# A two-block layer on one core: the last gate summed ahead of the expert gathers, the vector work around them rearranged

## The chip, the cores and the metric

The kernel runs on one core of a Trainium2 chip. The core has a matrix engine (TensorE, PE in the profile), a vector engine (VectorE, DVE), an engine for activation functions (ScalarE, ACT), a general one (GpSimd, POOL), and SyncE (SP), which here only issues transfers. Each runs its own list of instructions in order; semaphores order them against each other. 16 DMA engines move data between HBM and the on-chip memory. The metric is device microseconds of one execution, median of several.

## The reference, cut to what matters

Two transformer blocks over 256 tokens of width 1024, all in float32. The change touches the end of the first block, where a learned gate `gt2` scales the output of a mixture of tiny experts, and the first lines of the second:

```python
mod = (silu(c) @ w_mod + b_mod)               # one row of 6 x 1024
sh1, sc1, gt1, sh2, sc2, gt2 = jnp.split(mod, 6)
h = rmsnorm(x, ln_mix_g) * (1 + sc1) + sh1    # block 1: attention and convolution
...
x = x + gt1 * (mixed @ w_out)
h2 = rmsnorm(x, ln_ffn_g) * (1 + sc2) + sh2
x = x + gt2 * peer_ffn(h2, ...)
x = rmsnorm(x, ln_final_g)
h = rmsnorm_2(x, pre_norm_w)                  # block 2
q, k, v, ... = jnp.split(h @ w_in_2, ...)

def peer_ffn(xn, w_q, sub_keys, expert_u, expert_v):
    s = einsum('bshpd,hpkd->bshpk', q, sub_keys)      # scores of 2 x 128 half keys, 8 heads
    v_half, i_half = top_k(s, 16)                     # then the 16 best of the 256 sums
    experts = i1 * 128 + i2                           # 8 x 16 = 128 experts a token
    act = gelu(einsum('cd,ced->ce', xc, expert_u[ec]))
    return einsum('ce,ced->cd', softmax(top_s) * act, expert_v[ec])
```

## The kernel before, in words

The kernel is one program for five queues. Python code calls `PE(...)`, `V(...)`, `A(...)`, `G(...)` and `SP(...)` in one order; each call appends to its engine's list, with the tokens that it waits for in `after=`. So the order in which the code is written is the order on every engine. All instructions carry line 88, where the lists are emitted; they are told apart by their tiles.

Weights come in slabs of 1024 x 512 (2.1 MB, two DMA issues of 1 MB) into a ring of four slots, `W`. `plan` is the list of the slabs in the order of their use; `next_w` takes the next one, and `done_w(i, tok)` issues the load of slab i + 4 once `tok` has fired. These issues stand in SP's queue in the order of the calls.

The 12 slabs of `w_mod` give the row `mod`. Slabs 0 to 3 are done at the start by TensorE and VectorE. Slabs 6, 7, 8, 9 (shift and scale of the second norm) and 4, 5 (gate 1) are summed by POOL in `mod_sum`, called from `mod_next`: multiply the slab by the eight columns of silu(c), then add halves, quarters, eighths, so that a column sum over the 128 partitions is left; TensorE does that with a matmul against ones, into columns (`mod_cols_sum`, one column per matmul) or into a row on all partitions (`mod_row_mm`). Slabs 10 and 11 (gate 2) are left for later: `mod_row` multiplies them on TensorE, 8 matmuls of 512 columns each.

Then the stages around the change:

- up to about 200 us: norm, projections, first-block attention of the first 128 tokens ("half 0"), convolution (`conv_step`: one product and four operations of two operands of 128 x 128 per feature block and half), `attn_mm`, `q_norm1` and `q_norm2` (norm of the new x), `q_project`, and the first parts of `route`, a generator that finds the experts of a token's heads in small VectorE instructions. `keysT` goes to the half of `hT` that is free by then.
- the gather stage, 203 to 915 us: loop `for p in range(P)`, 128 pairs of gathers. A gather (`fetch`) brings, by indirect DMA from POOL's queue, 128 rows of 8 KB: the experts' u and v for a pair of positions of 64 tokens. VectorE takes the product with x over u (`ttr`, CUSTOM_DVE_ANT_0, accumulating), ScalarE takes the gelu and the weight and spreads it to a diagonal, TensorE adds diagonal times v to `E` (`combine`). A buffer is free when TensorE has used it; there are 5 buffers at first, 7 after some 17 pairs. Between the pairs stand the route parts, `advance(routes[0], 6 if p < 17 else 8)` of them, and the steps of `half1`: attention of the second 128 tokens, among them `weigh`, which multiplies the softmax of four heads by a factor per token and head. A gather of head h needs the CAST to `idx` of that head.
- half 0's output is complete after pair 63. From then on `x2_steps(0, ...)` is advanced by one step a pair: gate and add to x, final norm, pre-norm of block 2. Its transposes follow, and `qk_project` at p = 86, 92, 98 and 104 does the q and k projections of block 2 for half 0, 8 matmuls of 512 columns each; `rope` follows at p = 112.
- the tail: `x2_steps(1, ...)` for half 1, its projections, and the rest of block 2, in which TensorE is nearly always busy.

## Time and profile before

| | us |
|---|---|
| median of 3 runs | 1398.42 (1397.94 to 1399.48) |
| the profiled execution | 1404.89 |
| its span | 1403.1 |
| PE / DVE / ACT / POOL busy | 1154.9 / 743.8 / 485.0 / 363.9 |
| DMA, mean over the span | 270 GB/s, 378.7 MB |
| gathers | 256, 268.45 MB, median 11.3 us from issue to landing |

The profile is of one execution, a little slower than the median of the plain runs. Busy time on POOL is mostly the issuing of gathers. PE is busy where a matmul is under way, which says little on its speed: its granted clock, PEclk, is a mean of the stretch. In a timeline a row reads: start, duration, engine, line, operation, out<-in, shape, count, and in brackets the idle time ahead of it with what ended it. A row of VectorE or POOL can be long because the instruction waited for something that isn't a semaphore: its recorded duration then grows.

### The profile page before, as it was taken

What the parts mean: (1) busy time and instruction counts of PE and PEld (TensorE: products, weight loads), DVE (VectorE), ACT (ScalarE), POOL (GpSimd) and SP (SyncE); (2) the same over time, 40 slices, a digit from 0 to 9 for tenths busy, and PEclk for the clock granted to TensorE, in tenths of its full rate; (3) what the DMA queues carried; (4) which work ended last, traced back from release to release, by engine and by line L of the source; (5) the groups of instructions that cost most, each with busy time, mean ns of one, the idle gap of its engine ahead of it and who ended that gap; (6) DMA issues with size and microseconds to landing.
All of it is one profiled execution on the core that took longest, in us unless ns stands there. A gap on an engine that the chain in (4) does not pass through costs nothing.

```text
span 1403.1 us, 15272 instructions
## 1 busy us (share of the span) xinstructions
PE 1154.9 (82%) x5688; PEld 673.4 (48%) x5688; DVE 743.8 (53%) x1808; ACT 485.0 (35%) x1282; POOL 363.9 (26%) x285
## 2 busy tenths in 40 slices
PE   6999968878787678666677766779988998999997
PEld 2888653332342123111122211134867887899883
DVE  5132658888639994465444455430466567642111
ACT  1131124463424452344332233321577544113101
POOL 0888013333334543333343334300000000000000
PEclk9989967998898999899999998889999999999999
DMA  9965418999999999999999999914413131114130
GB/s 392 326 260 212 162 71 324 361 351 401 396 412 421 415 418 394 415 421 422 422 394 405 395 396 421 422 69 181 180 61 117 63 121 62 62 61 180 60 120 31
DMA packets 57094, 378.70 MB, mean 270 GB/s; under 512 B 7187, under 2 KB 10428, under 8 KB 11964
## 3 DMA queue, kind: packets, MB, share of 16 engines
q0 software_dynamic: 36864, 268.45, 47.2%
q1 hardware_dynamic: 19488, 107.23, 20.2%
q10 hardware_dynamic: 668, 2.04, 0.4%
q8 instruction: 45, 0.74, 0.2%
q14 instruction: 29, 0.24, 0.0%
HBM read 376.64 MB, written 1.06 MB: 269 GB/s over the span
## 4 chain that ended last, share of the span: by engine, by line
PE 51%; DMA 21%; DVE 17%; ACT 7%; issue 3%; POOL 1%; ACTq 0%; POOLq 0%; DVEq 0%
PE ps L88 51%; DMA AR<-in_puv,idx 20%; DVE AR L88 8%; DVE RT L88 3%; ACT L88 2%; ACT av L88 1%; DVE rowb L88 1%; DVE hT L88 1%; DVE acc L88 1%; POOL AR L88 1%; DMA X<-in_x 1%; ACT acc L88 1%; ACT rowb L88 1%; DVE junk L88 1%; ACT AR L88 1%
## 5 line engine op out<-in xcount | busy, mean ns | idle before, releaser
L88 PE MATMUL ps<-AR,acc 128*64 128x512 f32 x912 | 355.5, 704 | 172.0 <-ACT acc L88 171.0
L88 POOL DMA_INDIRECT AR<-in_puv,idx x256 | 271.3, 1060 | 491.7 <-PE ps L88 395.9
L88 PE MATMUL ps<-hT,W 128*128 128x256 f32 (+1 forms) x1472 | 318.0, 374 | 4.2 <-ACT rowb L88 3.0
L88 PEld LDWEIGHTS ps<-hT,W 128*128 128x128 f32 x1472 | 268.5, 198 | 54.7 <-issue 15.4
L88 PEld LDWEIGHTS ps<-AR,acc 128*64 128x64 f32 x912 | 85.9, 150 | 414.1 <-ACT acc L88 335.3
L88 DVE CUSTOM_DVE_ANT_0 AR<-AR,mixT 128x1024 f32<-128x1024 f32 x128 | 156.9, 1228 | 155.1 <-DMA AR<-in_puv,idx 154.9
L88 DVE CUSTOM_DVE_ANT_0 AR<-AR,tok 128x1024 f32<-128x1024 f32 x128 | 153.0, 1220 | 58.4 <-DMA AR<-in_puv,idx 58.3
L88 ACT ACTIVATE av<-av 128x1 f32<-128x1 f32 x256 | 51.3, 200 | 314.2 <-DVE av L88 314.0
L88 ACT ACT_TABLE_LOAD x104 | 133.4, 1283 | 12.8 <-DVE PT L88 11.0
L88 PE MATMUL ps<-W,hT 128*128 128x512 f32 (+3 forms) x288 | 98.0, 498 | 0.8 <-ACT hT L88 0.8
L88 ACT ACTIVATE acc<-fold,av 128x64 f32<-128x64 f32 x228 | 79.3, 348 | 7.4
L88 ACT ACTIVATE av<-av,gwp 128x1 f32<-128x1 f32 x256 | 75.4, 295 | 8.3
L88 PEld LDWEIGHTS ps<-W,hT 128*128 128x128 f32 x288 | 48.6, 194 | 49.1 <-issue 47.8
L88 ACT ACTIVATE PT<-ps 128x512 f32<-128x512 f32 (+1 forms) x44 | 21.6, 496 | 122.2 <-PE ps L88 121.6
L88 PE MATMUL ps<-AR,mixT 128*64 128x512 f32 x112 | 46.6, 747 | 20.9 <-ACT mixT L88 20.8
L88 ACT ACTIVATE AR<-ps 128x512 f32<-128x512 f32 (+5 forms) x51 | 22.9, 467 | 117.9 <-PE ps L88 117.8
L88 PE MATMUL ps<-AR,W 128*128 128x256 f32 x256 | 57.5, 381 | 0.0
L88 POOL TENSOR_TENSOR W<-W,st 128x4096 f32<-128x4096 f32 x6 | 42.1, 7016 | 47.1 <-DMA W<-in_w_mod 47.1
L88 PEld LDWEIGHTS ps<-AR,W 128*128 128x128 f32 x256 | 48.2, 190 | 6.6
L88 PE MATMUL ps<-AR 64*64 64x15 f32 (+4 forms) x416 | 49.7, 291 | 0.3
L88 PEld LDWEIGHTS ps<-AR 64*64 64x64 f32 (+2 forms) x416 | 39.9, 199 | 9.4 <-issue 2.7
L88 POOL TENSOR_TENSOR W<-W 128x2048 f32<-128x2048 f32 (+1 forms) x12 | 42.7, 3561 | 0.9
(231 smaller groups left out, 1092.3 us busy)
## 6 DMA issues: line engine op xcount, KB each, us to landing
W<-in_w_in SPq DMA_DIRECT2D x50, 1024.0 KB, 6.9
W<-in_w_mod SPq DMA_DIRECT2D x24, 1024.0 KB, 11.7
W<-in_w_out SPq DMA_DIRECT2D x4, 1024.0 KB, 5.9
W<-in_wq SPq DMA_DIRECT2D x4, 1024.0 KB, 8.1
AR<-in_puv,idx POOLq DMA_INDIRECT x256, 11.3
W<-in_wba SPq DMA_DIRECT2D x4, 1024.0 KB, 6.1
W<-in_wbb SPq DMA_DIRECT2D x4, 1024.0 KB, 7.0
W<-in_wo SPq DMA_DIRECT2D x4, 1024.0 KB, 6.0
```

The costliest lines, as they stand in the source:

```text
L88: ins = f(*args, **kw)
```

## The change

- Gate 2 is summed by POOL like the others. Its two slabs move in `plan` ahead of those of w_out and wq, `mod_next` is called twice more, around the DMA of the keys, with R_G2 as the buffers. Their column sums go to TensorE with those of the other four, and only then come the second norm's shift and scale. The row on all partitions is made later by `spread_g2`, from the 8 columns, four matmuls of 128 columns for each half of the row; the row broadcast from HBM goes.
- `mod_sum` works in pieces of 1024 elements a partition instead of up to 4096.
- `feat`, `token` and `q_project` wait, for each of the eight k, only for that piece of hT.
- `weigh` of half 1: the product is done by four ScalarE copies with a scale.
- Five route parts a pair instead of six for p < 17.
- `x2_steps` takes the sums of squares of x and of x times the final row from ScalarE, and the pre-norm directly from the raw product; the first half of the columns starts when its own matmuls are done.
- The q and k projections of half 0 come in pieces of two k, one a pair, from the pair on at which x is ready.

```diff
         for (a, n), m in zip(((0, 512), ..., (2328, 512)), (6, 7, 8, 9, 4, 5)):
             plan += [(w_in, a, n), (w_mod, m * 512, 512)]
+        plan += [(w_mod, 10 * 512, 512), (w_mod, 11 * 512, 512)]
         plan += [(w_out, 0, 512), (w_out, 512, 512), (wq, 0, 512), (wq, 512, 512)]
-        for n in (10, 11):
-            plan.append((w_mod, n * 512, 512))
...
-            t = G(gtt, w[:, :, :], w[:, :, :], cs.unsqueeze(2).to_broadcast([P, 8, 512]), MUL, after=[t_w, t_cs])
-            t = G(gtt, w[:, 0:4, :], w[:, 0:4, :], w[:, 4:8, :], ADD, after=[t])
-            t = G(gtt, w[:, 0:2, :], w[:, 0:2, :], w[:, 2:4, :], ADD, after=[t])
+            part = [w[:, 2 * k:2 * k + 2, :] for k in range(4)]
+            ts = [G(gtt, part[k], part[k], cs[:, 2 * k:2 * k + 2].unsqueeze(2).to_broadcast([P, 2, 512]), MUL, after=[t_w, t_cs])
+                  for k in range(4)]
+            t1 = G(gtt, part[0], part[0], part[1], ADD, after=ts[0:2])
+            t2 = G(gtt, part[2], part[2], part[3], ADD, after=ts[2:4])
+            t = G(gtt, part[0], part[0], part[2], ADD, after=[t1, t2])
             t = G(gtt, buf, w[:, 0, :], w[:, 1, :], ADD, after=[t] + free)
...
+        def spread_g2(n, after):
+            b = ps.take()
+            for j in range(4):
+                t = PE(mm, b.t[:, j * 128:j * 128 + 128], g2c[:, 4 * n + j:4 * n + j + 1].to_broadcast([P, P]), ident,
+                       start=True, stop=True, after=b.old + [t_g2c])
+            e = A(act, R_G2[:, n * 512:n * 512 + 512], b.t[:, :], ACT.Copy, after=[t] + after)
...
+        def of_k(t_r, k):
+            return t_r[k:k + 1] if len(t_r) == 8 else t_r
...
-            stage[u, "e"] = V(tt_, pu_, pu_, sm2[:, u, 4:8].unsqueeze(2).to_broadcast([P, 4, nk]), MUL, after=[t])
+            if a == 0:
+                stage[u, "e"] = V(tt_, pu_, pu_, sm2[:, u, 4:8].unsqueeze(2).to_broadcast([P, 4, nk]), MUL, after=[t])
+                return
+            for j in range(4):
+                stage[u, "e"] = A(act, pu_[:, j, :], pu_[:, j, :], ACT.Copy, scale=sm2[:, u, 4 + j:5 + j], after=[t])
...
+        mod_next()
         t_keys = {0: SP.dma(nc.sync.dma_start, s_k, kT_sb[0], keys3, after=[...])}
+        mod_next()
...
+        for n in range(2):
+            t_mg2 = mod_cols_sum(b2, 16 + 4 * n, *t_ms[6 + n])
...
-        sh2, sc2, t_m2 = mod_affine(b2, t_mc[3], 24, V_LNF, 16)
+        sh2, sc2, t_m2 = mod_affine(b2, t_mg2, 24, V_LNF, 16)
+        g2c = modc[:, 32:40]
+        t_g2c = V(tt_, g2c, b2.t[:, 16:24], PV[:, V_BMOD + 40:V_BMOD + 48], ADD, after=[t_mg2, t_pc])
...
         def x2_steps(a, t_acc, free):
             for n in range(2):
-                t = V(tt_, junk[:, c], E[a][n].t[:, :], R_G2[:, c], MUL, after=[t_acc] + t_g2 + ([t] if n else free))
+                t = V(tt_, junk[:, c], E[a][n].t[:, :], R_G2[:, c], MUL, after=[t_acc[n]] + t_g2 + free)
                 t = V(tt_, X[:, a, c], X[:, a, c], junk[:, c], ADD, after=[t])
+                t_sum.append(A(act, PT[:, 1, 0:512], X[:, a, c], ACT.Square, accum_out=sums[:, 0, n:n + 1], ...))
+                t = V(tt_, junk[:, c], X[:, a, c], R_LNF[:, c], MUL, after=[t, t_rows[0]])
+                t_sum.append(A(act, PT[:, 1, 512:1024], junk[:, c], ACT.Square, accum_out=sums[:, 1, n:n + 1], ...))
-            t = V(ttr, junk[:, :], X[:, a, :], X[:, a, :], 1.0 / D, EPS, MUL, ADD, r1, after=[t])
...
-            advance(routes[0], 6 if p < 17 else 8)
+            advance(routes[0], 5 if p < 17 else 8)
...
-                load_row(3, [t_idx[1, 7], t_gw[1, 7]])
-                for n in range(2):
-                    t_g2.append(mod_row(3, n))
+                spread_g2(0, [t_idx[1, 7], t_gw[1, 7]])
...
-            if p in (86, 92, 98, 104):
-                m = (p - 86) // 6
-                qk_project("qk"[m % 2], 0, m // 2, [t_tp, t_gw[1, 7]])
+            if t_hb and len(qk_done) < 16:
+                m, k0 = divmod(len(qk_done), 4)
+                qk_done.append(qk_piece("qk"[m % 2], m // 2, 2 * k0, [t_tp, t_gw[1, 7]]))
```

Three places in the instruction lists. On TensorE, behind `attn_mm` of half 0 (`W,mixT`), stand the column sums (`K,RT` and `K,rowb`), the sums for the convolution's norm (`AR,K`) and the transposes of q_norm2 (`K,tok`). Before:

```order
L88 MATMUL ps<-W,mixT 128x512 x16
L88 MATMUL ps<-K,RT 128x1 x12
L88 MATMUL ps<-K,rowb 128x1 x4
L88 MATMUL ps<-AR,K 128x128 x4
L88 MATMUL ps<-K,tok 128x128 x8
```

Now:

```order
L88 MATMUL ps<-W,mixT 128x512 x16
L88 MATMUL ps<-K,RT 128x1 x12
L88 MATMUL ps<-K,rowb 128x1 x12
L88 MATMUL ps<-AR,K 128x128 x4
L88 MATMUL ps<-K,tok 128x128 x8
```

Eight more one-column matmuls, those of the two gate-2 sums, stand ahead of the norm. On VectorE, pairs 6 to 8 of the gather stage; `ISA AR,av` is the product with a gathered buffer, two a pair, `CAST idx` writes the experts of head 1, which pair 8 is the first to need. Before, behind the sixth pair:

```order
L88 ISA AR,av<-AR,tok 128x1024
L88 ISA av 128x1
L88 ISA AR,av<-AR,tok 128x1024
L88 ISA av 128x1
L88 TENSOR_TENSOR rowb<-ps,acc 128x512 x2
L88 TENSOR_REDUCE sm<-rowb 128x4
L88 MAX RT<-ps 128x8
L88 MATCH_REPLACE rowb<-RT,ps 128x128 x4
L88 CAST idx<-ps 128x2x8
```

Now, behind the eighth:

```order
L88 MAX RT<-ps 128x8
L88 MATCH_REPLACE rowb<-RT,ps 128x128 x4
L88 ISA AR,av<-AR,tok 128x1024
L88 ISA av 128x1
L88 ISA AR,av<-AR,tok 128x1024
L88 ISA av 128x1
L88 CAST idx<-ps 128x2x8
```

The cast of head 1 moved back by two pairs. On TensorE in the second half of the gathers (`AR,acc`: combine, 4 matmuls a gather pair in each output bank's turn; `W,hT`: projection), before and now, one piece of the difference:

```order
-L88 MATMUL ps<-W,hT 128x512 x8
-L88 MATMUL ps<-AR,acc 64x512 x24
-L88 MATMUL ps<-W,hT 128x512 x8
-L88 MATMUL ps<-AR,acc 64x512 x92
+L88 MATMUL ps<-W,hT 128x512 x2
+L88 MATMUL ps<-AR,acc 64x512 x4
+L88 MATMUL ps<-W,hT 128x512 x2
+L88 MATMUL ps<-AR,acc 64x512 x4
```

Groups of eight are now groups of two, with one pair's combine between them.

## Rows read from the trace of the kernel before

**Rows 1.** The page: transfer rate in 40 slices of 35 us.

```profile
GB/s 392 326 260 212 162 71 324 361 351 401 396 412 421 415 418 394 415 421 422 422 394 405 395 396 421 422 69 181 180 61 117 63 121 62 62 61 180 60 120 31
```

**Rows 2.** Windows: stretch, length, busy (instructions) of each engine, PEclk, DMA, GB/s.

```profile
141.00:180.00 39.00, 36.58 (x151) 24.02 (x150) 25.69 (x69) 5.92 (x16) 0.30 (x1) 0.92 0.36 139
220.00:400.00 180.00, 145.05 (x621) 63.65 (x620) 137.91 (x378) 83.56 (x238) 64.26 (x60) 0.89 0.95 369
520.00:560.00 40.00, 33.55 (x104) 12.49 (x100) 22.30 (x46) 13.16 (x42) 12.71 (x11) 0.91 0.98 395
600.00:700.00 100.00, 64.52 (x168) 15.44 (x168) 55.92 (x95) 40.99 (x132) 38.51 (x40) 0.93 1.01 421
700.00:820.00 120.00, 91.39 (x248) 28.72 (x248) 56.35 (x91) 38.45 (x139) 45.82 (x46) 0.94 0.97 394
```

**Rows 3.** Timeline of SP's queue: start, length, issues.

```profile
340.17 13.53 SPq L88 DMA_DIRECT2D W<-in_w_mod  x4
```

**Rows 4.** Timeline of POOL: parts of two sums.

```profile
86.08 2.34 POOL L88 TENSOR_TENSOR W<-W 128x1024 f32<-128x1024 f32 x1
...
125.40 7.02 POOL L88 TENSOR_TENSOR W<-W,st 128x4096 f32<-128x4096 f32 x1 [3.87 <-DMA W<-in_w_mod]
...
140.04 1.26 POOL L88 TENSOR_TENSOR rowb<-W 128x512 f32<-128x512 f32 x1
```

**Rows 5.** Groups of POOL between 90 and 106 us: busy, mean ns | idle.

```profile
L88 POOL TENSOR_TENSOR W<-W 128x2048 f32<-128x2048 f32 x1 | 5.0, 5040 | 0.1
L88 POOL TENSOR_TENSOR W<-W 128x1024 f32<-128x1024 f32 x1 | 2.9, 2872 | 0.1
```

**Rows 6.** Timeline of VectorE beside POOL's sums.

```profile
92.83 3.99 DVE L88 TENSOR_TENSOR sm<-sm,AR 128x4 f32<-128x4 f32 x1
...
96.85 0.69 DVE L88 TENSOR_TENSOR tok<-tok,sm 128x512 f32<-128x512 f32 x1
...
128.24 4.20 DVE L88 TENSOR_TENSOR sm<-sm,AR 128x4 f32<-128x4 f32 x1
...
132.47 0.69 DVE L88 TENSOR_TENSOR tok<-tok,sm 128x512 f32<-128x512 f32 x1
```

**Rows 7.** Timeline of TensorE behind attn_mm of half 0.

```profile
157.50 13.90 PE L88 MATMUL ps<-W,mixT 128*128 128x512 f32 x32
171.24 2.73 PE L88 MATMUL ps<-K,RT 128*128 128x1 f32 x24
173.83 1.74 PE L88 MATMUL ps<-K,rowb 128*128 128x1 f32 x8
...
179.12 1.94 PE L88 MATMUL ps<-K,tok 128*128 128x128 f32 x8 [1.63 <-DVE tok L88]
```

**Rows 8.** Timeline of VectorE: the two-operand parts of one conv step.

```profile
145.14 0.74 DVE L88 SCALAR_TENSOR_TENSOR AR<-AR,PV 128x128 f32<-128x128 f32 x2
145.91 0.62 DVE L88 TENSOR_TENSOR AR<-AR 128x128 f32<-128x128 f32 x2
```

**Rows 9.** Timeline of TensorE: the first projection.

```profile
40.71 5.65 PE L88 MATMUL ps<-hT,W 128*128 128x256 f32 x17 [1.20 <-ACT hT L88]
```

**Rows 10.** Groups of VectorE: half 1's weight product.

```profile
L88 DVE TENSOR_TENSOR rowb<-rowb,sm 128x1024 f32<-128x1024 f32 x4 | 5.0, 1240 | 0.1
```

**Rows 11.** Timelines: head 1's cast, the issue behind it, a product of gather 15.

```profile
247.29 0.16 DVE L88 CAST idx<-ps 128x16 uint32<-128x16 f32 x1
...
249.51 0.94 POOL L88 DMA_INDIRECT AR<-in_puv,idx  x1 [0.55 <-PE ps L88]
...
254.78 1.22 DVE L88 CUSTOM_DVE_ANT_0 AR<-AR,tok 128x1024 f32<-128x1024 f32 x1
```

**Rows 12.** Timeline of TensorE: one q and k projection of half 0.

```profile
706.85 7.13 PE L88 MATMUL ps<-W,hT 128*128 128x512 f32 x16
```

**Rows 13.** Timelines: half 1's first square sum, and the tail's first projection.

```profile
921.82 1.23 DVE L88 CUSTOM_DVE_ANT_0 junk<-X 128x1024 f32<-128x1024 f32 x1
...
930.19 35.30 PE L88 MATMUL ps<-W,hT 128*128 128x512 f32 x76 [0.81 <-ACT hT L88]
```

More of the change, by code:

```diff
@@ L813, in q_project @@
                     t = PE(mm, b.t[:, j * 128:j * 128 + 128], w[:, k, q * 128:q * 128 + 128], hT[:, k, c],
-                           start=(k == 0), stop=(k == 7), after=b.old + [t_w] + t_hx[a])
+                           start=(k == 0), stop=(k == 7), after=b.old + [t_w, t_hx[a][k]])
             if js[-1] == 0:
@@ L1050, in build @@
         scores_add(4)
-        routes = [route(0, [])]
+        routes = [route(0, [t_mg2])]
         advance(routes[0], 1)
@@ L1167, in qk_project, with qk_piece @@
             t_rot.setdefault((kind, a), []).append(e)
+        qk_bank = {}
+        def qk_piece(kind, n, k0, free):
+            if (kind, n) not in wqk:
+                wqk[kind, n] = next_w()
+            i, w, t_w_ = wqk[kind, n]
+            if k0 == 0:
+                qk_bank[kind, n] = ps.take()
+            b = qk_bank[kind, n]
+            for k in (k0, k0 + 1):
+                t = PE(mm, b.t[:, :], hT[:, k, 0:P], w[:, k, :], start=(k == 0), stop=(k == 7),
+                       after=b.old + [t_w_, t_hb[0][k]])
+            if k0 == 6:
+                e = A(act, rot[kind, 0][:, n * 512:n * 512 + 512], b.t[:, :], ACT.Copy, after=[t] + free)
+                b.free = [e]
+                t_rot.setdefault((kind, 0), []).append(e)
         def rope(kind, a, free):
@@ L1200, in combine @@
                                 after=[e, t_fold] + dg_free[d] + ([late_t["dg"]] if "dg" in late_t else t_mc))))
+            ends = []
             for c in range(2):
@@ L1209, in combine @@
                         ring.append([n, [e]])
-            return e
-        ahead = []
+                ends.append(e)
+            return ends
+        ahead, qk_done = [], []
         h1 = half1()
@@ L1245, in build @@
                 routes.append(None)
-                load_row(3, [t_idx[1, 7], t_gw[1, 7]])
-                for n in range(2):
-                    t_g2.append(mod_row(3, n))
+                spread_g2(0, [t_idx[1, 7], t_gw[1, 7]])
+            elif len(routes) == 3 and len(t_g2) < 2:
+                spread_g2(1, [t_idx[1, 7], t_gw[1, 7]])
             if p == 63:
                 e_last = e
-            if p >= 63 and t_g2 and t_xb2[0] is None and not ahead:
+            if p >= 63 and len(t_g2) == 2 and t_xb2[0] is None and not ahead:
                 ahead = [x2_steps(0, e_last, [])]
@@ L1298, in build @@
         rope_turn("k", 0)
-        for _ in x2_steps(1, t_pelast, t_rot["k", 0]):
-            pass
+        last = x2_steps(1, e, t_rot["k", 0])
+        while t_xb2[1] is None:
+            advance(last, 1)
         t_xb = t_xb2[1]
@@ L1304, in build @@
         t_hball = t_hb[0] + t_hb[1]
+        advance(last, 9)
         for n in range(2):
```

49 lines of the change are left out of this document (32 added, 17 removed).

## The prediction

> **What bounds the kernel now.** I read the row of transfer rates over the span first [rows 1], then the windows [rows 2], then the timelines of the stages in which the change puts something. The span of 1403.1 us has three parts. Up to the first gather (202 us) TensorE works without a pause from 40.7 to 153 us and then waits in short steps. From there to 915 us the 256 gathers of 1 MB run: between 600 and 700 us the transfers move 421 GB/s, and the slices of the rate row from 420 to 910 us stand at 394 to 422, so here the DMA is the bound. Before it is reached, 220 to 400 us gives 369 GB/s, with VectorE busy 137.9 of 180 us; that is 180 x (1 - 369/421) = 22.2 us of transfer time lost. 520 to 560 loses 40 x (1 - 395/421) = 2.5 us, 700 to 820 loses 120 x (1 - 394/421) = 7.7 us [rows 2]. After 930 us TensorE is the bound to the end. So a delay ahead of the first gather is paid in full, a byte less in the middle is a gain in full, and an engine's work in the middle counts only through those three losses.
>
> **Part by part.**
>
> *1. The two last gate slabs leave the gather stage.* Before, four issues of 1.05 MB of w_mod stand there from 340 us [rows 3], and a row broadcast of 0.52 MB. 4 x 1.05 + 0.52 = 4.7 MB by 421 GB/s is 11.2 us. The 16 long matmuls of those slabs go too. They ran in one piece in the window 520 to 560, whose loss was 2.5 us; I take all of it. Term: -13.7 us.
>
> *2. The price: POOL now works from 141 to about 190 us, where it stood idle.* One sum takes 7.02 us for the multiplication, then adds of 2048, 1024 (2.34) and 512 (1.26), 125.40 to 141.30 in all, 15.9 us [rows 4]. In pieces the elements are the same: 4 x (7.02/4 + 0.09) + 3 x 2.43 + 1.3 = 15.9 us, with a start gap of some 0.09 us (0.07 to 0.09 in these rows); two more instructions' fixed parts may add half a us each. Three sums from 125.4 us end at 125.4 + 3 x 15.9 = 173 us if nobody is in the way. In the program order of TensorE the columns of the eleventh slab stand ahead of the sums for norm c1 and of the transposes of q_norm2. Before, the columns ended at 173.83 + 1.74 = 175.6 us, and the transposes began at 179.12 [rows 7]. Undisturbed, only eight more one-column matmuls come in: half of 173.83's group per slab (1.74 us for four), at its lower rate 0.9 us each, +1.8 us. That is the low end.
>
> It won't be undisturbed. In the trace a VectorE multiplication of 4 columns took 3.99 and 4.20 us instead of 0.17, and both ended within 0.05 us of the end of the POOL multiplication beside it; the other way round POOL's add of 2048 elements took 5.04 us, and that of 1024 took 2.87 instead of 2.34, when a VectorE product of two SBUF operands started 0.02 us ahead [rows 4 to 6]. So the two exclude each other. The Trainium skill says so ("SBUF — State Buffer", section "Who interferes with whom"): a VectorE operation with two SBUF inputs and a GpSimd one that reads SBUF block each other for the whole instruction; by this rule the trace agrees.
>
> What VectorE has of that kind between 125 and 175 us: eight conv steps of 0.74 + 0.62 = 1.36 us [rows 8], 10.9; two weight products of 512 columns and two adds to X of the same width at 0.69 [rows 6], 2.8; the mix of four times 128 columns, about as much as a conv step's four, 1.3; the square sum over 1024, 1.2 as in [rows 13]: 16.2 us. POOL has work all the time, so it ends at 173 + 16 = 189 us at the latest, if VectorE's goes first each time. Behind POOL's end: the last four columns 0.9, modc 0.5, the normalised x 0.8, a hop: transposes at 189 + 2.4 = 191.5 at most, 179.12 before, +12.4. VectorE's waits for pieces under way (1.8 to 2.4 us each, at each start of a run of such operations) come on top where TensorE waits for it: turn_p(3), the mixed columns of attn_mm, each once: +2 to +5. I take +15, with +1.8 and +27.5 (rival 1) as the ends. In SP's queue the first wq slab and the keys now stand behind POOL's sum of slab 10: issued at about 165 to 176 us, 12 us to land at most even with 3 MB at the 260 GB/s of the rate row's third slice, wanted from 196 on: hidden. The second wq slab follows slab 11, at about 190, and is wanted some 50 us later.
>
> *3. Per-k waits.* The first projection waits 1.20 us for all eight pieces of hT [rows 9]; with one piece it starts right behind the transposes: -1.1 us, carried on to 153 us because TensorE never pauses in between.
>
> *4. Half 1's weights and five parts a pair.* Up to pair 17 VectorE loses 17 route parts of 137.91/378 = 0.36 us [rows 2] = 6.1 us, and three or four products of 1.24 us [rows 10] = 4.5 us. Against it: the cast of head 1's indices moved from behind six pairs to behind eight. Gather 16 was issued at 249.51 us, 2 us behind that cast; now it needs the products of gathers 14 and 15 first, of which the second began at 254.78 [rows 11]. That is 256 + 0.3 instead of 249.5, less the 5 us or so that VectorE has gained by then: a gap of 2 us. From 10.6 us of work taken out of a stage that is 77% VectorE-bound I count -3; ends: -9 (all of it, within the 22 us lost there) and +6 (the gap without the gain). The 17 parts put off run behind pair 17.
>
> *5. The q and k projections in pieces of two k.* Four bursts of 7.1 us of TensorE [rows 12] become 16 of 1.7 us, one a pair, beside 64.52/20 = 3.2 us of its own in a pair of 5 us [rows 2]. They hold buffers up less: of 7.7 us lost I count -5.5; ends -7.7 and 0.
>
> *6. Raw sums at the end.* Ahead of the tail stood a square sum of 1.23 us, the product with the final row and a second square sum of the same size, two roots, and the tail's first matmul at 930.19 [rows 13]. Now two products over half the columns (0.69 us, as in [rows 6]) and ScalarE's squares take their place, saving about 1.5 us, and the first matmul waits for one piece of hT: 0.7. Term -2.2, ends -4 and 0.
>
> **Sum.** -13.7 + 15 - 1.1 - 3 - 5.5 - 2.2 = -10.5 us. The profiled execution, 1404.89 us (span 1403.1 and 1.8 around it), would take 1394.4. It lies 6.5 us above the median of the runs, 1398.42, so the forecast for the median is 1388 us. What can't be told from no change here is 0.2%, 2.8 us.
>
> **Rivals.**
>
> *Rival 1, slower: POOL's waiting piece goes first each time.* Place: 141 to 185 us. If the port is given in turn, every VectorE operation of that kind stands behind a fresh piece, and VectorE is late by all of POOL's work, 2 x 15.9 = 31.8 us, less some 4 of the 13 us that it idles in the 39 [rows 2] (the rest are waits that recur later): +27.5 instead of +15. TensorE then stands idle for some 20 us ahead of attn_mm and may go on at its lower level, which the windows show as a mean of 0.92 now [rows 2]; 16 k-steps of 0.87 us [rows 7] at half speed for a third of them is +4. Sum: -10.5 + 12.5 + 4 = +6: 1404 us. It decides from +26 us at the transposes. Against it: in both cases where VectorE had waited, its next product came 0.03 us later and went ahead of POOL's next instruction [rows 6]. For it: POOL needs 0.08 us to come back, so that shows nothing of a run of five. By the same page's sentence that issue order decides who blocks, the turn-taking follows, POOL having asked first. 27%.
>
> *Rival 2: hardly any collision.* If two-operand products with a per-partition scalar don't collide, or POOL falls in VectorE's idle 13 us of the 39 [rows 2], the transposes come at +2: -10.5 - 13 = -23.5, 1375 us. Against it: the four waits seen. 13%.
>
> *Rival 3: the middle does not give it back.* The bubble at pair 8 costs its 6 us and the pieces gain nothing: -10.5 + 9 + 5.5 = +4, 1402 with the full price, 1396 with half. Against it: VectorE has 0.36 us per part less to do. 12%.
>
> **How the numbers follow.** Forecast case 48%, 1388, its own range 1381 to 1395. Range over the cases: low 1375 (rival 2), high 1405 (rival 1). Faster: 46 + 13 + 2 = 61%; same: 2 of the forecast, 6 of rival 3, 5 of rival 1 = 13%; slower: 22 + 4 = 26%.
>
> **What would show it.** POOL's last sum ending at 186 to 192 us (179: rival 1; 174: rival 2). Transposes of q_norm2 at 191 to 196 us, first gather at about 216. Conv steps of VectorE with single waits of 1.5 to 2.4 us at the start of a run, not in each instruction. Last gather landing near 903 to 907 instead of 915. 700 to 820 us without the dip below 415 GB/s, no 7 us burst. One gap in the gathers ahead of number 16. Wrong would be the forecast if the conv steps show a wait in every operation, or if the gather stage, first issue to last landing, isn't shorter than the 712 us of now by 15 to 25 us.

## The result and the profile after

| | before | after |
|---|---|---|
| median of the runs on one chip, us | 1398.95 (1397.94 to 1401.21, 4 runs) | 1414.62 (1411.65 to 1415.31, 4 runs) |
| ratio to before, 95% interval | | 1.0104 (1.0086 to 1.0122) |
| the profiled execution, its span, us | 1404.89, 1403.1 | 1414.84, 1413.0 |
| PE / DVE / ACT / POOL busy, us | 1154.9 / 743.8 / 485.0 / 363.9 | 1150.4 / 759.5 / 500.1 / 397.8 |
| first gather issued, us | 202.06 | 225.29 |
| last product with a gathered buffer starts, us | 914.72 | 925.83 |

The change makes the kernel 1% slower; the forecast was 1388 us. One of the twelve runs of e8 below took 1571 us at a lower granted clock; the ratios leave it out. The rates over the span come first, as in [rows 1]:

```profile
GB/s 393 330 249 238 222 32 207 269 358 383 394 348 423 420 420 405 411 422 421 421 421 421 422 421 422 421 113 189 162 78 87 92 120 61 62 61 179 60 119 30
```

The sixth slice, at 32 GB/s, and the seventh are the gathers' later start. The stretch at 421 to 422 now runs through what was the dip of 394 to 405; a new hole of 348 stands in the twelfth slice, 388 to 424 us. The windows of [rows 2], after (columns: each engine's busy time and count, TensorE's granted clock, DMA share, GB/s):

```profile
141.00:180.00 39.00, 18.37 (x66) 11.93 (x65) 37.35 (x38) 4.86 (x13) 31.16 (x16) 0.69 0.59 229
220.00:400.00 180.00, 128.07 (x508) 53.97 (x506) 133.52 (x393) 88.33 (x236) 61.10 (x55) 0.83 0.87 343
520.00:560.00 40.00, 27.36 (x147) 10.66 (x147) 39.04 (x119) 20.73 (x58) 17.53 (x15) 0.96 1.01 410
700.00:820.00 120.00, 87.74 (x227) 21.75 (x224) 62.41 (x109) 41.31 (x146) 47.79 (x48) 0.96 1.01 421
```

From 141 to 180 us VectorE is busy 37.35 of 39 us with 38 instructions, where it was busy 25.69 us with 69 [rows 2]: its records have grown long. TensorE is busy 18.37 us instead of 36.58. That is the price. These are rows of VectorE there (here and below, rows are left out where the times jump):

```profile
142.60 1.25 DVE L88 TENSOR_SCALAR AR<-AR,PV 128x128 f32<-128x128 f32 x1
143.89 3.78 DVE L88 SCALAR_TENSOR_TENSOR AR<-AR,PV 128x128 f32<-128x128 f32 x2
147.70 4.66 DVE L88 TENSOR_TENSOR AR<-AR 128x128 f32<-128x128 f32 x2
152.49 2.23 DVE L88 TENSOR_TENSOR sm<-sm,AR 128x4 f32<-128x4 f32 x1
154.75 0.69 DVE L88 TENSOR_TENSOR tok<-tok,sm 128x512 f32<-128x512 f32 x1
171.45 1.63 DVE L88 TENSOR_TENSOR AR<-AR 128x128 f32<-128x128 f32 x2
173.31 0.74 DVE L88 SCALAR_TENSOR_TENSOR AR<-AR,PV 128x128 f32<-128x128 f32 x2
174.08 0.62 DVE L88 TENSOR_TENSOR AR<-AR 128x128 f32<-128x128 f32 x2
```

The conv step of 0.74 + 0.62 us [rows 8] takes 3.78 + 4.66; a product of 4 columns takes 2.23. At 173 us, when POOL is done, the long records end. POOL in the same stretch, with the first gather behind:

```profile
140.03 7.49 POOL L88 TENSOR_TENSOR W<-W,st 128x1024 f32<-128x1024 f32 x4
147.48 7.21 POOL L88 TENSOR_TENSOR W<-W 128x1024 f32<-128x1024 f32 x3
154.77 1.82 POOL L88 TENSOR_TENSOR rowb<-W 128x512 f32<-128x512 f32 x1
156.56 7.58 POOL L88 TENSOR_TENSOR W<-W,st 128x1024 f32<-128x1024 f32 x4
164.11 7.16 POOL L88 TENSOR_TENSOR W<-W 128x1024 f32<-128x1024 f32 x3
171.34 1.26 POOL L88 TENSOR_TENSOR rowb<-W 128x512 f32<-128x512 f32 x1
225.29 1.11 POOL L88 DMA_INDIRECT AR<-in_puv,idx  x1 [52.69 <-DVE gw L88]
```

The two sums take 140.03 to 172.60 = 32.6 us, 0.8 more than twice 15.9: POOL hardly waited. Nearly all of the waiting is VectorE's. The one exception in these rows is VectorE's product at 154.75 us: it keeps its 0.69 us, and POOL's add, which starts 0.02 us behind it, takes 1.82 us instead of 1.26. TensorE's rows, which answer to [rows 7]:

```profile
155.50 1.12 PE L88 MATMUL ps<-K,tok 128*128 128x128 f32 x4 [7.16 <-DVE tok L88]
174.85 2.05 PE L88 MATMUL ps<-AR,K 128*128 128x128 f32 x8 [12.78 <-DVE AR L88]
178.94 13.90 PE L88 MATMUL ps<-W,mixT 128*128 128x512 f32 x32
201.38 1.94 PE L88 MATMUL ps<-K,tok 128*128 128x128 f32 x8 [1.63 <-DVE tok L88]
```

TensorE waits 7.16 us for turn_p(3) and 12.78 us for half 0's conv output, whose sums start at 174.85 us, where they started at 154.82 before. Before:

```profile
154.82 1.13 PE L88 MATMUL ps<-AR,K 128*128 128x128 f32 x8
```

The low granted clock of this stretch falls on the matmuls from there to attn_mm: they take 178.94 - 174.85 = 4.09 us, at a clock of 0.64, instead of 157.50 - 154.82 = 2.68 [rows 7]. In attn_mm itself the granted clock is 1.00, and it takes 13.90 us as before (columns as above):

```profile
178.90:192.80 13.90, 13.90 (x35) 6.21 (x34) 8.99 (x27) 0.00 (x0) 0.00 (x0) 1.00 0.02 8
```

The transposes of q_norm2 come at 201.38 us (179.12 before). In a second trace of the kernel after (a2 below) they come at 204.16: the last column sums, 24 records, take 5.26 us there at a granted clock of 0.50, and 2.82 us at 1.00 here.

The gather stage I read by the starts of VectorE's products with gathered buffers, counted from the first (us; "before" and "after" each have a second trace, from the runs below):

| product | before | before, 2nd | after | after, 2nd |
|---|---|---|---|---|
| first, from the span's start | 207.7 | 205.1 | 231.0 | 233.8 |
| 48 | 157.4 | 154.6 | 161.4 | 165.0 |
| 54 | 171.7 | 166.3 | 181.2 | 183.6 |
| 104 | 312.1 | 306.1 | 320.0 | 323.8 |
| 112 | 344.6 | 338.8 | 338.1 | 341.9 |
| 160 | 462.7 | 458.0 | 458.8 | 462.1 |
| 224 | 629.4 | 624.1 | 617.8 | 621.1 |
| 255 | 707.0 | 702.5 | 694.8 | 698.2 |
| from there to the span's end | 488.4 | 486.9 | 487.2 | 485.8 |

Two steps of it are gains: 104 to 112 takes 18.1 us instead of 32.6 to 32.7, and 160 to 224 takes 159.1 instead of 166.1 to 166.6 (the q and k pieces). In the first, the gate slabs' own loads are not what is gone: they had been issued at 340 us [rows 3]. Here stood their matmuls and, behind them, four loads of w_in for the slots that these held. Before (TensorE, SP):

```profile
535.42 14.00 PE L88 MATMUL ps<-W,st 128*128 128x512 f32 x32
542.59 7.67 SPq L88 DMA_DIRECT2D W<-in_w_in  x4
```

After, the eight loads of w_in are all issued between 368 and 447 us:

```profile
368.37 78.66 SPq L88 DMA_DIRECT2D W<-in_w_in  x8
```

Both the 14 us of TensorE and the 4.2 MB are gone from this place, and no run tells what each is worth. One step is a loss that I had not foreseen: up to 104 the stage is 8 to 18 us later, of it 4 to 8 us between the products 48 and 54 alone.

A candidate for the first part of that loss is the one bubble I had priced, at gather 16 (VectorE's row, then POOL's; they answer to [rows 11]):

```profile
281.04 0.17 DVE L88 CAST idx<-ps 128x16 uint32<-128x16 f32 x1
```

```profile
272.34 0.94 POOL L88 DMA_INDIRECT AR<-in_puv,idx  x1 [4.05 <-PE ps L88]
281.98 0.94 POOL L88 DMA_INDIRECT AR<-in_puv,idx  x1 [8.71 <-DVE RT L88]
```

POOL stands 8.71 us for the indices (0.55 before [rows 11]). The second part, products 48 to 54, is a wait of VectorE:

```profile
400.50 1.22 DVE L88 CUSTOM_DVE_ANT_0 AR<-AR,tok 128x1024 f32<-128x1024 f32 x1
408.03 0.19 DVE L88 CAST idx<-ps 128x32 uint32<-128x32 f32 x1 [6.30 <-PE ps L88]
```

and TensorE and ScalarE, in the same microseconds:

```profile
393.20 1.09 PE L88 MATMUL ps<-K,PT 128*128 128x128 f32 x8
400.39 4.47 PE L88 MATMUL ps<-AR,acc 128*64 128x512 f32 x8 [6.09 <-ACT acc L88]
404.79 2.83 PE L88 MATMUL ps<-hT,W 128*128 128x128 f32 x16
407.55 0.42 PE L88 MATMUL ps<-RT,K 128*64 128x16 f32 x8
```

```profile
393.68 2.90 ACT L88 ACTIVATE hT<-ps,modc 128x128 f32<-128x128 f32 x8 [3.79 <-PE ps L88]
396.59 1.28 ACT L88 ACT_TABLE_LOAD   x1
397.89 0.23 ACT L88 ACTIVATE gw<-gw 128x32 f32<-128x32 f32 x1
398.13 1.28 ACT L88 ACT_TABLE_LOAD   x1
```

The spreading of the indices (RT,K) stands in TensorE's order behind a pair's combine and a piece of the q projection (hT,W). The combine had waited 6.09 us for ScalarE. VectorE's products for that pair were done by 394.8 us, but ScalarE first copied the transposed columns into hT and then did an activation of the gate weights (gw), with a table load of 1.28 us ahead of it and one behind; it came to the pair at 399.43 us. With six parts (e3 below) that activation stands at 375.48 us, well ahead of this place, and the combine waits 2.79 us. Then VectorE waits 6.30 us for TensorE, and POOL stands 8.65 us for a free buffer.

The tail begins 939.49 - 925.83 = 13.7 us behind the last product's start, 930.19 - 914.72 = 15.5 before [rows 13]:

```profile
939.49 15.75 PE L88 MATMUL ps<-W,hT 128*128 128x512 f32 x33
```

### The profile page after: what moved, and what is told of

Its sections match the earlier page's. It is cut to its first block, busy times and chain, and to the rows that moved or that the text cites. A ratio compares the mean times of both kernels' runs of the same rounds, so it can differ in the third digit from the quotient of the medians.

```text
span 1413.0 us, 15352 instructions
## 1 busy us (share of the span) xinstructions
PE 1150.4 (81%) x5688; PEld 669.1 (47%) x5688; DVE 759.5 (54%) x1807; ACT 500.1 (35%) x1318; POOL 397.8 (28%) x325
## 4 chain that ended last, share of the span: by engine, by line
PE 49%; DMA 22%; DVE 18%; ACT 7%; issue 3%; POOL 1%; ACTq 0%; POOLq 0%; DVEq 0%
PE ps L88 49%; DMA AR<-in_puv,idx 21%; DVE AR L88 10%; DVE RT L88 3%; ACT L88 2%; ACT av L88 1%; DVE rowb L88 1%; DVE acc L88 1%; ACT acc L88 1%; DMA X<-in_x 1%; POOL AR L88 1%; ACT rowb L88 1%; ACT AR L88 1%; DVE tok L88 1%; DVE junk L88 0%
## 5 line engine op out<-in xcount | busy, mean ns | idle before, releaser
L88 PE MATMUL ps<-AR,acc 128*64 128x512 f32 x912 | 353.8, 684 | 168.2 <-ACT acc L88 166.3
L88 PE MATMUL ps<-hT,W 128*128 128x256 f32 (+1 forms) x1472 | 317.9, 374 | 3.1 <-ACT rowb L88 3.0
L88 PEld LDWEIGHTS ps<-AR,acc 128*64 128x64 f32 x912 | 82.7, 146 | 410.6 <-ACT acc L88 327.5
L88 PE MATMUL ps<-W,hT 128*128 128x512 f32 (+3 forms) x288 | 100.7, 500 | 0.0
L88 POOL TENSOR_TENSOR W<-W,st 128x1024 f32<-128x1024 f32 x32 | 60.6, 1925 | 43.1 <-DMA W<-in_w_mod 43.1
L88 POOL TENSOR_TENSOR W<-W 128x1024 f32<-128x1024 f32 x24 | 56.3, 2359 | 1.1
```

What stands on the lines that cost most here:

```text
L88: ins = f(*args, **kw)
```

## The experiments

Theory: while POOL sums, each VectorE instruction with two SBUF operands waits for the end of a POOL instruction, POOL hardly waits, and VectorE's work of this stretch is done only when POOL's is. Rivals: TensorE's clock or the new order; the pieces; the loads that were moved forward. For the gather stage: the five parts, or the weights on ScalarE. Ratios are to the kernel before, in runs on the same chip, with 95% intervals; "before" had medians of 1398.9 to 1402.2 us there.

**e1: the gate slabs back on TensorE, all else kept.**

```diff
-        plan += [(w_mod, 10 * 512, 512), (w_mod, 11 * 512, 512)]
         plan += [(w_out, 0, 512), (w_out, 512, 512), (wq, 0, 512), (wq, 512, 512)]
+        for n in (10, 11):
+            plan.append((w_mod, n * 512, 512))
...
-        mod_next()
```

Both new calls of `mod_next` go, and `spread_g2` gives way to `load_row` and `mod_row`.

> The changed kernel with one part undone: the last two gate slabs are again taken as row products on TensorE in the gather stage, and GpSimd makes no sums after 141 us. All other edits stay. Turn-taking theory (each two-operand VectorE instruction waits for one fresh GpSimd instruction, and only those sums make the wait): conv steps back at 0.74 and 0.62 us, transposes of q_norm2 at 177 to 179 us instead of 201.4, first gather at 201 instead of 225.3; the gather stage loses the 13 to 14 us that the slabs had freed, so the time is 1414.6 - 22.3 + 13.7 = 1406, or less if the pairs around the slabs lose less (1396 to 1406). Rival A, the collision is only half of the 22 us and the rest is the clock level or the order of the new instructions on TensorE: transposes at 188 or later, time 1410 or more. Rival B, the early gather stage was late because of the delayed start (it ran against other transfers): then its 7.9 us against the kernel before go as well and the time is below 1396.

Measured: 1398.33 us, ratio 0.9990 (0.9974 to 1.0006). First gather at 198.99 us. VectorE's conv step:

```profile
143.26 0.74 DVE L88 SCALAR_TENSOR_TENSOR AR<-AR,PV 128x128 f32<-128x128 f32 x2
144.03 0.62 DVE L88 TENSOR_TENSOR AR<-AR 128x128 f32<-128x128 f32 x2
```

The 26 us ahead of the gathers go with the slabs' move to POOL, so the other edits did not make them. At the transposes (201.38 against 175.60 us) they are 21.9 us of VectorE's lateness at the conv output (174.85 against 152.93), 1.4 us of TensorE at the lower clock ahead of attn_mm, and 2.5 us behind it, most of that the eight more one-column matmuls. The products 104 to 112 take 32.5 us again. The time is inside the 1396 to 1406 us expected. The rest of the edits together are worth nothing here: what they gain late, the stage loses before product 104 (322.3 us).

**e2 and e15: the kernel before, with the gate slabs on POOL alone.** The edit is e1's diff turned round, with `mod_sum` in pieces; the q and k projections, six parts and the weights stay as before. It was run twice.

> The kernel before with one part of the change alone: the last two gate slabs go to GpSimd, in pieces. Turn-taking theory: transposes of q_norm2 at about 201 us (179.1 before), the gather stage 13.7 us shorter, so 1399 + 22.3 - 13.7 = 1407.5 us (1405 to 1411). Rival A: the delay comes from the other edits too (smaller conv pieces, per-k waits): transposes before 195 us and a time near 1399. Rival B: the delay is not given back at all in this kernel, whose q and k projections stand at fixed pairs: 1420.

> The kernel before with the last two gate slabs on GpSimd alone, repeated. By the sum of the measured stages (+25 us to the first gather, -14.3 us for the slabs) it should take 1410 us; the five runs gave 1420.7. If those runs were typical of this kernel: ratio 1.013 to 1.018 again. If they were not: 1.006 to 1.010.

Measured: 1420.7 us, ratio 1.0157 (1.0133 to 1.0181), and 1417.5 us, 1.0117 (1.0090 to 1.0145). First gathers at 226.04 and 226.45. So the start costs what it costs in the changed kernel, +25.5 us against the mean of before's two traces. Of the 14 us that the slabs give back (104 to 112 takes 18.3 and 18.9 us), the first trace keeps 11.4 over the whole stage and the second only 4.9, since its products up to 104 come 316.6 - 309.1 = 7.5 us later than before's mean. The first time is the one of rival B (1420), but not by its mechanism: the steps 104 to 112 show that the slabs do give their 14 us back. By the medians this kernel is 6 to 10 us slower than the start and the slabs account for. Why the middle is slower in some executions of it I can't say; before's own two traces differ by 6 us there. That stays open.

**e3: six route parts instead of five in the changed kernel.**

```diff
-            advance(routes[0], 5 if p < 17 else 8)
+            advance(routes[0], 6 if p < 17 else 8)
```

> The changed kernel with six route parts a pair before pair 17 instead of five, all else kept. Theory: five parts cost time in the early gather stage, since the indices of head 1 come one or two pairs later (gather 16 issued at 282 us, 9 us later against the first gather than before) and the parts put off fall on the pairs from 25 on, where VectorE was 92% busy: the first 128 gathers shorten by 4 to 8 us and the time is 1407 to 1411. Rival: the loss there comes from ScalarE's scaling of the weights or from the order of the pieces, and six parts change nothing within 0.2% (1412 to 1417), or cost what they add to VectorE, up to 6 us (1420).

Measured: 1405.24 us, ratio 1.0053 (1.0031 to 1.0075), where the changed kernel has 1.0104 and, on another chip, 1.0082. The first 128 products take 368.4 us instead of 378.0 and 381.0, a little more than the 4 to 8 us expected. Products 48 to 54 take 12.2 us instead of 19.8. Its rows at the place, TensorE's and then VectorE's:

```profile
391.08 1.09 PE L88 MATMUL ps<-K,PT 128*128 128x128 f32 x8
392.10 0.42 PE L88 MATMUL ps<-RT,K 128*64 128x16 f32 x8
395.31 2.73 PE L88 MATMUL ps<-AR,acc 128*64 128x512 f32 x8 [2.79 <-ACT acc L88]
```

```profile
392.71 1.22 DVE L88 CUSTOM_DVE_ANT_0 AR<-AR,tok 128x1024 f32<-128x1024 f32 x1
393.86 0.18 DVE L88 CAST idx<-ps 128x32 uint32<-128x32 f32 x1
```

The spreading stands ahead of the combine and of the projection, the combine waits 2.79 us instead of 6.09, and the cast waits for nothing.

**e5 and e13: both undone** (e1's and e3's edits together), run twice.

> The changed kernel with two parts undone: the last two gate slabs again as row products on TensorE in the gather stage, and six route parts a pair before pair 17. The scaling on ScalarE, the pieces of the q and k projections, the per-k waits and the raw sums stay. If the two effects add (gate slabs on GpSimd cost 16.3 us by the first experiment, five parts cost 9.4 us by the third), the time is 1414.6 - 16.3 - 9.4 = 1389 us (1386 to 1392). Rival: five parts hurt only because the start was late and the kernel's later pairs were then loaded with the gate work; then 1395 to 1399.

> The kernel of the fourth experiment once more (gate slabs in the gather stage, six parts, weights on ScalarE), as the base for the next two: ratio to the kernel before 0.990 (0.988 to 0.993).

Measured: 1388.95 us, ratio 0.9904 (0.9872 to 0.9936), and 1387.66, 0.9896 (0.9869 to 0.9922). The two effects add up as expected, and the ratio is below those of e1 and e3.

**e9: six parts up to pair 7, then five, on e5.**

```diff
-            advance(routes[0], 6 if p < 17 else 8)
+            advance(routes[0], 6 if p < 8 else 5 if p < 17 else 8)
```

> The kernel of the fourth experiment (gate slabs on TensorE in the gather stage, six route parts), with six parts only up to pair 7 and five from pair 8 to 16. Nine parts are put off behind pair 17 instead of seventeen, but the indices of gather 16 come as early as with six. If the loss of five parts (8 to 9 us up to the 128th gather) comes from the late indices, this one is at 1389, within 2 us of the fourth experiment. If it comes from the parts put off, about half of it is paid: 1393 to 1394.

Measured: 1392.62 us, ratio 0.9932 (0.9907 to 0.9957), where e7 on the same chip had 0.9891: the intervals overlap, the time alone doesn't decide. The trace shows which step belongs to what: POOL waits 1.27 us ahead of gather 16 and product 48 comes at 154.0 us, as early as in any; 48 to 54 takes 19.7 us, as in all kernels with parts put off. So the parts put off, nine as well as seventeen, make the slow step at 48 to 54, and the late indices don't. What this costs in all the trace doesn't tell: by product 104 e9 is at 313.8 us, its base at 313.2 (e5) and 312.9 (e13), which had come to product 48 some 4 us later. What the late indices cost by themselves stays open too. With them product 32 comes at 106.8 to 109.8 us in after, a2, e1 and e4, but at 103.8 in e12 and 100.7 in e6b below, though POOL stands 9.0 and 9.9 us for them there; without them it comes at 98.8 to 104.8.

**e7 and e14: half 1's weights back on VectorE, on e5.** Run twice.

```diff
-            if a == 0:
-                stage[u, "e"] = V(tt_, pu_, pu_, sm2[:, u, 4:8]..., MUL, after=[t])
-                return
-            for j in range(4):
-                stage[u, "e"] = A(act, pu_[:, j, :], pu_[:, j, :], ACT.Copy, scale=..., after=[t])
+            stage[u, "e"] = V(tt_, pu_, pu_, sm2[:, u, 4:8]..., MUL, after=[t])
```

> The kernel of the fourth experiment, with the softmax weights of half 1 scaled on VectorE again (one product of 4 x 128 columns instead of four on ScalarE). Theory: the scaling on ScalarE gains nothing, since the gather stage up to gather 128 takes 369 to 370 us with it and 363 to 369 without: 1389, within 2 us of the fourth experiment. Rival (my prediction's term): VectorE's 1.24 us products come back onto a loaded engine, three or four of them: 1391 to 1393. Second rival: it is faster without, 1385 to 1387, because a weight was ready later on ScalarE.

> The same with half 1's weights on VectorE. Theory (the scaling on ScalarE gains nothing and costs a little, because a weight is ready later): ratio to the kernel before 0.988 to 0.990, at or up to 3 us below the one before. Rival (the scaling on ScalarE gains what it takes off VectorE): 2 us or more above it.

Measured: 1386.93 us, 0.9891 (0.9865 to 0.9917), and 1388.16, 0.9896 (0.9865 to 0.9926); e13, on the chip of the second, has 0.9896 too. The scaling on ScalarE is worth nothing that these runs can tell, within 4 us.

**e12: five parts with the weights on VectorE** (e1 with e7's edit, so with the gate slabs on TensorE).

> The same as the second, with five parts a pair before pair 17. If the five parts alone are the loss: 8 to 9 us above the second, 1396, as the first experiment lies above the fourth. If five parts were only bad together with the later weights: within 3 us of the second.

Measured: 1397.78 us, ratio 0.9983 (0.9969 to 0.9996), 9.6 us above e14 on its chip. The five parts alone are the loss. In the traces 6.1 us of it are there by product 104 (317.9 against 311.8), 6.0 of these between the products 48 and 54 (18.4 against 12.4).

**e6b: POOL fills instead of summing** (the changed kernel with five parts; the last two gates' arithmetic is left out).

```diff
+            if len(t_ms) >= 6:
+                t = t_w
+                for k in range(16):
+                    t = G(nc.gpsimd.memset, w[:, 2 * (k % 4):2 * (k % 4) + 2, :], 0.0, after=[t, t_cs])
+                t = G(nc.gpsimd.memset, buf, 0.0, after=[t] + free)
...
```

> The changed kernel, leaving out the arithmetic of the last two gate slabs' sums (six sums keep theirs): GpSimd fills the same tiles with zeros in seventeen instructions per slab instead of multiplying and adding. It only writes SBUF. It tells whether what VectorE waits for is GpSimd's being busy or its reading of SBUF. Theory (only instructions that read SBUF take the port): conv steps at 0.74 and 0.62 us while GpSimd is busy, transposes of q_norm2 at 176 to 183 us, time 1392 to 1397. Rival (any GpSimd instruction on SBUF takes it): VectorE's two-operand instructions each last one fill longer, 1 to 2 us, and the transposes come at 190 or later.

Measured: 1388.72 us, ratio 0.9919 (0.9890 to 0.9948); first gather at 202.08. POOL's row, then VectorE's beside it:

```profile
140.15 16.09 POOL L88 MEMSET W<- 128x1024 f32 x16
```

```profile
145.55 0.67 DVE L88 TENSOR_SCALAR AR<-AR,PV 128x128 f32<-128x128 f32 x1
146.26 0.74 DVE L88 SCALAR_TENSOR_TENSOR AR<-AR,PV 128x128 f32<-128x128 f32 x2
147.03 0.62 DVE L88 TENSOR_TENSOR AR<-AR 128x128 f32<-128x128 f32 x2
```

POOL is busy without a pause for 33 us, and the two-operand instructions take their 0.74 and 0.62 us. It isn't POOL's being busy that VectorE waits for; what the fills leave out is the reading of SBUF (and the arithmetic). The transposes come at 178.59 us, 22.8 and 25.6 us earlier than in the two traces with sums, with the same loads moved forward and as many column sums on TensorE: that is the collision, with what it costs TensorE in clock. The time is 3 us below the range expected. Against e1's 175.60 us, 3.0 us stay, which are the eight more one-column matmuls and a lower clock behind them. The one-operand TENSOR_SCALAR is longer, mostly 0.65 to 0.71 us, where e1 has 0.28. Both agree with the Trainium skill ("SBUF — State Buffer", section "Who interferes with whom"): two SBUF inputs on VectorE contend with a GpSimd instruction that reads SBUF and not with one that only writes, while a `tensor_scalar` in its two-port mode contends with either. That this TENSOR_SCALAR runs in that mode, no row says.

**e4: whole instructions; and a2, the changed kernel once more on the same chip.**

```diff
-            ts = [G(gtt, part[k], part[k], ..., MUL, after=[t_w, t_cs]) for k in range(4)]
...
+            t = G(gtt, w[:, :, :], w[:, :, :], cs.unsqueeze(2).to_broadcast([P, 8, 512]), MUL, after=[t_w, t_cs])
+            t = G(gtt, w[:, 0:4, :], w[:, 0:4, :], w[:, 4:8, :], ADD, after=[t])
+            t = G(gtt, w[:, 0:2, :], w[:, 0:2, :], w[:, 2:4, :], ADD, after=[t])
```

> The changed kernel with GpSimd's sums in whole instructions (one product of 4096 elements, adds of 2048, 1024 and 512) as before the change, all else kept. Turn-taking with work conserved: VectorE waits for longer pieces but fewer of them, and TensorE's transposes of q_norm2 come when both engines' work is done: first gather at 225 to 230 us, the time within 4 us of the changed kernel (1413 to 1419). Rival (pieces made it worse, since each fresh piece takes one VectorE instruction hostage): first gather at 215 or earlier, 1405 or less. Rival (pieces were what kept it bearable): 235 or later, 1423 or more.

> The changed kernel, unchanged, on the chip of the two comparisons above and for a second trace: 1412 to 1416 us. The first gather at 224 to 227 us again, the first 128 gathers in 378 us (within 3), the last 64 in 116 to 117.

Measured: 1414.93 us, ratio 1.0081 (1.0053 to 1.0109), against 1415.83, 1.0082 (1.0054 to 1.0111); first gathers at 228.45 and 228.38. So a2's start was 1.4 us later than the range expected; its column sums ran at a clock of 0.50. VectorE in e4:

```profile
145.51 7.03 DVE L88 SCALAR_TENSOR_TENSOR AR<-AR,PV 128x128 f32<-128x128 f32 x2
152.57 8.35 DVE L88 TENSOR_TENSOR AR<-AR 128x128 f32<-128x128 f32 x2
```

POOL in e4:

```profile
138.37 7.02 POOL L88 TENSOR_TENSOR W<-W,st 128x4096 f32<-128x4096 f32 x1
145.47 6.92 POOL L88 TENSOR_TENSOR W<-W 128x2048 f32<-128x2048 f32 x2
```

The second sum, from 153.68 us, goes the same way. The waits are fewer and longer, and the conv output comes at 174.96 us, at 174.85 and 174.51 with pieces: the size of the pieces is worth nothing.

**e8: the gate's columns on TensorE, ahead of the gathers** (the changed kernel with six parts; 32 one-column matmuls a slab).

```diff
+        def gate_cols(n, w3):
...
+            for j in range(4):
+                for k in range(8):
+                    t = PE(mm, b.t[:, j:j + 1], w[:, k, j * 128:j * 128 + 128], cs[:, k:k + 1], start=(k == 0), stop=(k == 7), ...)
```

> The changed kernel with six route parts, and with the columns of the last two gate slabs made by TensorE straight from the slabs (32 one-column matmuls per slab) where the changed kernel lets GpSimd sum them; GpSimd has no sums after 141 us, the loads stay ahead of the gathers. 64 one-column matmuls at 0.114 us are 7.3 us of TensorE before the first gather, partly in its waits. Theory (GpSimd's hold on the SBUF port is the whole cost of moving the slabs): no long VectorE instructions after 141 us, first gather at 200 to 207 us, gather stage as short as in the third experiment (686 us from first to last dot, 707 before), so 1399 + 3 - 21 - 1.2 = 1380 us (1375 to 1385). Rival (loading the slabs early is itself a cost, through late w_out and wq slabs): first gather at 212 or later, 1388 or more.

Measured: 1403.87 us, ratio 1.0033 (1.0012 to 1.0055); first gather at 219.32, the stage 687.6 us long from the first product to the last. TensorE's two groups:

```profile
145.50 8.95 PE L88 MATMUL ps<-st,W 128*128 128x1 f32 x64
184.32 13.65 PE L88 MATMUL ps<-st,W 128*128 128x1 f32 x64
```

The stage went as expected, the start didn't, through my own price: the profile's count is two records to a matmul (x24 there, x12 in the instruction list), so 0.114 us was half a matmul. 32 of them took 8.95 us at a granted clock of 0.79, and 13.65 at 0.50 behind the transposes, 22.6 in all instead of 7.3, and nearly all on the path. The start is 22.4 us later than e5's 196.97, as much as those 22.6, so the earlier loads cost nothing that shows; but as a cure it is dear.

**b2: the kernel before once more.**

> The kernel before, unchanged, for a second trace. The first one was profiled at 1404.89 us, 6 us above the kernel's median, and the sum of the differences of the two traces (+9.9 us) is 6 us short of the difference of the medians (+15.7). If the 6 us lie in one stage of the first trace, this one (1395 to 1402 us expected) shows that stage shorter: either the gathers between 200 and 400 us or those between 700 and 820 us; if they are spread, every stage differs by 1 to 2 us.

Measured: 1396.22 us, span 1394.4. Of the 8.7 us between the two traces of the same kernel, 2.6 lie ahead of the first product, 6.0 between products 0 and 104, 1.5 of them come back later, and 1.5 lie in the tail. Ahead of the gathers the seven traces without POOL's last sums and with the other edits (e1, e5, e7, e9, e12, e13, e14) spread further, from 194.4 to 199.7 us at the first gather. So a trace pins a term of this kernel to some 5 us ahead of the gathers, and to 6 in their first part.

## Why the prediction was wrong

It named the right places and put the likeliest case on the wrong side of its rival 1, which is what happened (27%, 1404 us). The measured 1414.6 us lie above its whole range, 1375 to 1405. By its own terms, in us:

| term | forecast | measured | from |
|---|---|---|---|
| 1 slabs leave the gather stage | -13.7 | -14.5 | products 104 to 112 |
| 2 POOL's sums, collision | +15 | +29.5 | first gather: 225.3, 228.4, 226.8 (after, a2, e3) against 194.4 to 199.7, mean 197.3 (e1, e5, e7, e9, e12 to e14) |
| 3 per-k waits | -1.1 | -3.4 | first gather without POOL's sums, mean 197.3, against before's mean 200.7, with a spread of 5.3 |
| 4 five parts, ScalarE's weights | -3 | +10 | product 104: 320.0 to 323.8 against 306.1 and 312.1; e12 against e14, e14 against e13 |
| 5 q and k pieces | -5.5 | -7 | products 160 to 224 |
| 6 raw sums | -2.2 | -3 | last product to the end: mean 485.0 in thirteen traces with the edit, 488.1 in four without |
| sum | -10.5 | +11.6 | measured +11.5 and +14.5 by the two ratios, +13.7 and +15.7 by the medians |

The two traces after are 16.6 us longer on the mean than the two before. What the table's sum lacks of that is in term 4, which is 12.8 us in these four traces at product 104, and in 1.7 us between the products 112 and 160.

*The step that failed most is term 2's choice.* The prediction laid the two engines' work end to end, which gives POOL's end at 189 us "if VectorE's goes first each time", and named POOL's end at 179 as the sign of the rival. POOL ended at 172.6, nearest to the sign given for rival 2, while the time went the way of rival 1: this sign could not tell the rivals apart. POOL isn't delayed at all. The sentence for rival 1, that each VectorE operation stands behind a fresh piece, holds nearly word for word. Its price, 27.5 us, is near the 24.9 us by which the transposes came later on the mean of two traces each, and that is in part luck: VectorE's lateness, which it put at 31.8 less 4 us, was 20.8 to 22.0 us at the conv output (174.85, 174.51 and 173.64 in after, a2 and e3, 152.84 in e6b). For VectorE has work for a part of POOL's 32.6 us in any case (from the first conv step to the last it needs 9.8 us in e1 and 32.1 in after), and is late only by the rest. What came on top is TensorE's: 1.4 to 2.5 us more ahead of attn_mm at the lower clock, 1.8 us for the eight more one-column matmuls, and up to 2.4 us where these ran at half the clock. So the extra 4 us for the clock came, but not in attn_mm, which took 13.90 us as before.

What speaks against the rival in the prediction was the two rows in which VectorE's next product came 0.03 us after POOL's end [rows 6]; the prediction itself said that these show nothing of a run of five, and still gave them weight. The other two rows it had, POOL's 5.04 and 2.87 us [rows 5], are delays of some half a microsecond, against VectorE's 3.99 and 4.20. The asymmetry stood in the rows. The prediction's own signs of being wrong both held: nearly every two-operand instruction of the conv steps waited, and the stage from the first gather to the last product's start is 700.5 and 703.6 us, 8 us shorter than before's 712.7 and 708.1 on the mean, not 15 to 25.

*The second is term 4, and no rival had it whole.* Rival 3 had the bubble at pair 8, and POOL did stand 8.71 us there; some 4 to 5 us of that stay in four traces and none in two (e12, e6b). The rest is the sentence "the 17 parts put off run behind pair 17", which had no price. They move the spreading of two heads' indices behind a combine and a q projection on TensorE, and that combine behind two table loads on ScalarE: products 48 to 54 take 18.4 to 19.8 us in all seven traces with parts put off, 11.7 to 14.2 in the ten without. The gain that stood against it, 17 parts and three products taken from a VectorE 77% busy, did not show: parts put off are not parts saved, they are due before pair 32 in any case, and the weights' 1.24 us on VectorE were in nobody's way (e7, e14).

*Terms 1, 3, 5 and 6 came out right*, within some 2 us each, and for term 3 that is within the spread of the starts. Term 1 had its size right; of its reasons, the loads taken out at 340 us show no gain there, and all of it comes where the slabs' matmuls had stood. To carry the sum from a trace 6.5 us above the median over to the median was fair: the second trace shows that slowness spread over all stages. The range's upper end, 1405, was the rival's time; it held the collision's price, but not with term 4's on top.

## What to carry over

- Before work goes to POOL, ask what VectorE does beside it. If POOL's instructions read SBUF and VectorE's take two SBUF operands, VectorE's work is done only when POOL's is, in whatever pieces: here it was some 22 us late beside 32.6 us of POOL's work, and the first gather some 26 us. Filling costs nothing of the kind. Price it by POOL's end less the time at which VectorE would have been done, and add what TensorE, left idle, loses in clock.
- Work put off on a loaded engine comes back at a place of its own: read which round trips between two engines (a spread, a transpose, its evacuation) the shift moves, and what then stands ahead of them in the other's order.
- The best kernel here keeps the gate slabs on TensorE among the gathers, six parts, the per-k waits, the q and k pieces and the raw sums: 0.990 of the kernel before, medians of 1386.9 to 1389.0 us (e5, e13, and e7, e14 with the weights on VectorE).

## What the hardware showed that I had not expected

- The two engines do not share the wait: with both asking all the time, VectorE's two-operand instructions of 0.31 to 0.37 us last until about the end of the POOL instruction under way (1.9 to 2.4 us each in pieces, up to 6.99 us whole), and POOL's two sums take 32.6 us instead of 31.8. The Trainium skill ("SBUF — State Buffer", section "Who interferes with whom") says that whoever issues first gets the ports for the whole instruction and the other blocks; in these rows that is POOL nearly each time, and no run here shows a case with VectorE ahead for long.
- The one-operand TENSOR_SCALAR over 128 columns waits as well: 1.25 to 1.65 us beside sums in pieces, mostly 0.65 to 0.71 beside fills, 0.28 alone. The four-column product waits like the large ones; RECIPROCAL (0.17 us) and an operation on PSUM and one SBUF operand (0.68) did not.
- TensorE's lower clock was paid neither in the waits nor in the large block behind them but in the small matmuls around it: the same 24 records of one column take 2.82 us at a granted clock of 1.00 and 5.26 at 0.50.
- Two executions of one unchanged kernel differ by 6 us in the first 104 gathers, though its tail repeats within 1.5 us.
